# Attention scores of two heads at once, in the two row halves of the array, and block loops written out

## The chip, the core and the metric

The kernel runs on one core of a Trainium2 chip. The metric is the device time of one launch in microseconds (us); the kernel before takes 2647.19 us, the median of three runs (2647.19 to 2650.35). A core has TensorE (PE in the profile; its weight loads are shown apart as PEld), VectorE (DVE), ScalarE (ACT), GpSimd (POOL) and SyncE (SP, which issues the DMAs here). Each runs its own instructions in its own order, and they wait for each other by semaphores. TensorE reads SBUF and writes PSUM, which has 8 banks of 512 float32 values per partition.

## The reference

Two layers, 1024 tokens, model width 1024, heads of 64 channels. Each layer:

```
h = rms_norm(x);  q, k, v = h @ w_in               (three groups of heads)
A: 4 heads, neighbourhood of 8 x 16 on a 16 x 64 grid, learned relative bias
B: 6 query heads on 2 key/value heads, +-128 tokens, ALiBi, a sink per head
C: 6 heads, windows 128, 512, 2048 with dilation 1, 4, 16, ALiBi, mixed by softmax denominators
x = x + concat(rms_norm(A), rms_norm(B), rms_norm(C)) @ w_out
x = x + (silu(h @ w_gate) * (h @ w_up)) @ w_down     (h = rms_norm(x), hidden width 2816)
```

q and k are RMS-normalised per head. For a head, scores = q k^T / 8 + bias, masked; p = softmax(scores); output = p v. All is float32.

## The kernel before

A layer has three parts: the projections, the attention, and output projection with feed-forward part. The change is in the attention, which runs through bodies of tiles. A tile is one head with 128 queries. Four bodies of 24 tiles do the dilated branches 16 and 4 of C (kinds c3 and c2). Then come eight blocks of 128 tokens of 16 tiles each: tiles 0 to 5 are the heads of B, 6 to 11 those of C (dilation 1), 12 to 15 those of A. The first block (b0) and the last (b7) have narrower key windows: 256 keys for B and A and 192 for C, where the six inner blocks have 384 and 256. `plan` lists the bodies; `run` emits them, and the inner blocks 2 to 5 come from a hardware loop (Fori), with their addresses worked out in registers.

A tile goes through these steps:
- `score` (TensorE, L1984): one float32 matmul, queries stationary, keys moving, into a PSUM slot. The trace shows each float32 matmul as two (load, matmul) pairs. QK holds the transposed q and k, two heads of 64 channels in the 128 partitions. The full 128 rows are contracted, so the other head's half of the queries has to be zero: QS holds copies of the queries with zeros in it. For the blocks GpSimd makes these copies (`stage`, L1815); they count up the semaphore `staged`. There are two score slots of two banks (`score2`).
- `tmin` (VectorE, L1381): table minus score, with the row's minimum, into T.
- `exponential` (ScalarE, L1007): in T.
- `unit` (TensorE, L2000): two or three 128 x 128 transposes of T, into bank 4 or 5 by turns. It waits until the unit two before it has been copied out of that bank. For each block but the first, four more units transpose the normalised output Y of the block before: at tiles 8, 9, 11 and 15.
- `copy_unit`: copies bank 4 to PT (VectorE, L1517) or bank 5 (ScalarE, L1019); for Y to QK (L1521, L1023).
- `weigh` (TensorE, L2022): two matmuls of 65 columns per 128 keys, into bank 6 or 7.

The order is written out by hand. TensorE's `pe_body` does for tile s: the score of tile s + 2, the units of tile s, the weighted sum of tile s - 2. VectorE's does for tile s: the copy, the minimum of tile s + 2, then a piece of side work for the block before (`late_finish`, `own_finish`: merging the branches of C, denominators, squares for the norm). ScalarE's does the exponential of tile s + 1, then the copy of tile s. GpSimd raises the mean squares to the power -1/2 (`mean_powers`, L1822), between its copies.

Of the kernel before, what the change touches and what calls it, by code (L numbers as in the profile page):

```python
# [19 lines left out]
P = 128  # L20


def build_program(nc, x, gains, w_in, rpb, w_out, w_gu, w_down, out):
    depth, D = w_in.shape[0:2]
    S = x.shape[1]
    MT = S // P
# [38 lines left out]
    with ctx:  # L65
# [90 lines left out]
        QS = sb("QS", [P, 16, P], F32, "Q")  # L156
# [46 lines left out]
        score2 = [psum[:, 1024 * i:1024 * i + 1024] for i in range(2)]  # L203
# [104 lines left out]
        with nc.Fori(0, depth) as l, ExitStack() as layer:  # L308
# [170 lines left out]
            for kind, rounds, b0 in (("c3", 2, 0), ("c2", 2, 0), ("b0", 1, 0), ("mid", 5, 1), ("b6", 1, 6),  # L479
                                     ("b7", 1, 7)):  # L480
                bd = body(kind, b0, t0, u0, g0, q0)
                nt, nu = n_tiles(bd), len(events(bd))
                ng, nq = (4, 8) if kind in ("c3", "c2") else (3, 6)
                plan.append((bd, rounds, (nt, nu, ng, nq)))
                t0, u0, g0, q0 = t0 + rounds * nt, u0 + rounds * nu, g0 + rounds * ng, q0 + rounds * nq
# [11 lines left out]
            def run(eng, program):  # L497


                for n, entry in enumerate(plan):  # L500
# [5 lines left out]
                    elif dilated(entry[0]):  # L506
                        program(entry[0], shifted(entry, 1), before)
                        program(shifted(entry, 1), after, entry[0])
                    else:
                        program(entry[0], shifted(entry, 1), before)  # L510
                        with loop(eng, 1, rounds) as r:
                            program(shifted(entry, r), shifted(entry, r + 1), shifted(entry, r - 1))
# [13 lines left out]

            def keys(bd, s):

                k, b, (w, _) = bd["kind"], bd["i"], width(bd, s)
                if k == "c3":  # L530
                    return [KS[:, s // 6 % 2, s % 6 // 2, 0:128]]
                if k == "c2":
                    return [KS[:, s // 6 % 2, s % 6 // 2, 0:192]]
                if s < 6:
                    return [QK[:, T_BK, bass.ds(0 if k == "b0" else b * P - P, w)]]
                if s < 12:
                    return [QK[:, T_CK + (s - 6) // 2, bass.ds(0 if k == "b0" else b * P - 64, w)]]
                return [QK[:, T_AK + (s - 12) // 2, bass.ds(0 if k == "b0" else b * P - P, w)]]
# [707 lines left out]
            def _(dve):  # L1246
# [111 lines left out]
                def tmin(bd, s, gate):  # L1358
# [21 lines left out]
                    tt, sc = T[:, s % 4, off:off + w], score2[s % 2][:, 0:w]  # L1380
# [387 lines left out]
            def _(pool):  # L1768
# [15 lines left out]
                def stage(bd, before, q, after_powers):  # L1784

                    k, i = bd["kind"], bd["i"]
                    nh = 4 if q == 2 and not dilated(bd) else 6
                    q2 = q % 2 if dilated(bd) else q

                    if dilated(bd) and q >= 2:  # L1790
                        pool.wait_ge(scored, bd["T"] + 6 * (q - 1))
                    elif before is not None:
                        last = 6 * q + 18 if dilated(before) else 6 * q + nh
                        pool.wait_ge(scored, before["T"] + min(last, n_tiles(before)))
# [4 lines left out]
                    after_powers()  # L1799
                    carrier()  # L1800
                    if dilated(bd):
                        dst = QS[64:128, 6 * q2 + 1:6 * q2 + 7:2, :]
                        kd = KS[:, q2, :, :]
                        if k == "c3":
                            dst = dst.rearrange("p t (r j) -> p t r j", r=2)
                            kd = KS[:, q2, :, 0:128].rearrange("p t (r j) -> p t r j", r=2)
                        g.tensor_copy(dst, dilated_rows(bd, T_CQ, q, P)[64:128]).then_inc(staged, 1)
                        pool.wait_ge(staged, done + 1)
                        carrier()
                        g.tensor_copy(kd, dilated_rows(bd, T_CK, q, 192)).then_inc(staged, 1)  # L1810
                    else:
# [6 lines left out]
                def mean_powers(fam, b, copies):  # L1818
                    pool.wait_ge(gvar_s[fam], b + 1)
                    pool.wait_ge(staged, copies)  # L1820
# [4 lines left out]
                def pool_body(bd, nxt, before):  # L1825

                    b = bd["i"]
                    if dilated(bd):
                        first = bd["kind"] == "c3" and before is None
                        for q in range(4):  # L1830
                            stage(bd, before, q, (lambda: pool.wait_ge(v_ones, 3 if bd["kind"] == "c2" else 2))
                                  if q == 0 else (lambda: None))
                            if first and q == 1:
                                pool.wait_ge(stat, 2 * QT)
                                pool.wait_ge(staged, 4)
                                g.memset(VC[0:64, 0, :, :], 0.0).then_inc(v_ones, 1)
                        return
                    if bd["kind"] == "b0":
                        pool.wait_ge(qk_s, 2 * QT)

# [360 lines left out]
```

## Time and profile before

| | |
|---|---|
| median of 3 runs | 2647.19 us |
| the profiled execution | 2648.14 us, span 2646.4 us |
| granted TensorE clock, mean | 0.981 of full speed |
| busy: PE, DVE, ACT, POOL | 95%, 65%, 41%, 21% of the span |
| attention blocks, layer 1 | about 370 to 555 us |
| one inner block | about 24 us |

The profile page gives each engine's busy time over the whole span, which mixes stages with different limits. Timelines give the start and duration of instructions, those of one line in a row taken together; the durations of matmuls overlap, so that the distance between starts, not the duration, is what a step costs. In brackets stands the idle time ahead of an instruction, and what ended it.

### The profile page before, as it was taken

The numbers are of one execution on the slowest core, as the hardware profiler recorded it, in microseconds if no ns is written. First come the engines' busy times: TensorE is split into PE (matmuls) and PEld (weight loads), VectorE is DVE, ScalarE is ACT, GpSimd is POOL, SyncE is SP. The second block draws the span as 40 slices with busy tenths as digits, with TensorE's granted clock in tenths as the row PEclk, the third lists the DMA queues.
The fourth block names the chain that finished last, engine by engine and source line by source line (L and its number), as shares of the span: only waits on it lengthen the run. The fifth ranks groups of instructions, "written<-read, shape, count | busy, mean of one in ns | idle before, by whom it ended". The sixth has DMA issues, their size and how long they took to land.

```text
span 2646.4 us, 37474 instructions
## 1 busy us (share of the span) xinstructions
PE 2514.2 (95%) x12576; PEld 2109.7 (80%) x12576; DVE 1732.3 (65%) x3358; ACT 1074.3 (41%) x2138; POOL 563.7 (21%) x510
## 2 busy tenths in 40 slices
PE   6999899989899999999989999999898999999997
PEld 5987788878688888878778878888687888888786
DVE  4388667763855555689844986677547555556896
ACT  3333655553522232334343336555444222223342
POOL 1000222100444444200000003221004545441000
PEclk9999999989999999999989999999899999999999
DMA  4311520022222221612232115100331222227023
GB/s 179 94 46 40 120 66 19 13 104 84 80 72 92 76 80 48 224 71 92 68 127 84 44 39 130 51 17 19 107 107 58 86 82 86 61 59 278 13 92 120
DMA packets 229528, 220.19 MB, mean 83 GB/s; under 512 B 48880, under 2 KB 190576, under 8 KB 229360
## 3 DMA queue, kind: packets, MB, share of 16 engines
q1 hardware_dynamic: 229360, 218.07, 26.1%
q8 instruction: 90, 1.47, 0.2%
q14 instruction: 78, 0.64, 0.1%
HBM read 169.96 MB, written 48.06 MB: 82 GB/s over the span
## 4 chain that ended last, share of the span: by engine, by line
PE 45%; DVE 3%; ACT 1%; issue 1%; POOL 0%; DVEq 0%; ACTq 0%; POOLq 0%
PE psum L2121 15%; PE psum L1900 6%; PE psum L1902 6%; PE psum L1901 6%; PE psum L1984 4%; PE psum L2022 3%; PE psum L2000 2%; DVE X L1703 0%; DVE OPL_t L1632 0%; DVE XN L1267 0%; DVE WL L1626 0%; PE psum L2078 0%; PE psum L1948 0%; PE psum L1949 0%; PE psum L1913 0%
## 5 line engine op out<-in xcount | busy, mean ns | idle before, releaser
L2121 PE MATMUL psum<-OPH_t,WH 128*128 128x512 f32 x704 | 276.7, 393 | 17.0 <-DVE WL L1626 7.5
L2121 PE MATMUL psum<-OPH_t,WL 128*128 128x512 f32 x704 | 275.7, 392 | 0.0
L2121 PE MATMUL psum<-OPL_t,WH 128*128 128x512 f32 x704 | 275.6, 392 | 0.0
L1626 DVE TENSOR_TENSOR WL<-RAW,WH 128x512 fp32r<-128x512 f32 x132 | 162.4, 1230 | 160.3 <-ACT WH L1140 160.3
L1900 PE MATMUL psum<-BH,AH 128*128 128x512 f32 x616 | 242.1, 393 | 11.3 <-DVE BL L1695 10.8
L1901 PE MATMUL psum<-BL,AH 128*128 128x512 f32 x616 | 240.9, 391 | 0.0
L1902 PE MATMUL psum<-BH,AL 128*128 128x512 f32 x616 | 240.9, 391 | 0.0
L1007 ACT ACTIVATE T<-T,G 128x192 f32<-128x192 f32 (+3 forms) x352 | 166.3, 473 | 170.4 <-DVE G L1381 167.1
L1870 POOL TENSOR_TENSOR WS<-RAW 128x512 f32<-128x512 f32 x88 | 157.5, 1790 | 238.5 <-PE psum L1902 195.6
L2121 PE MATMUL psum<-OPH_b,WH 128*128 128x512 f32 x528 | 205.8, 390 | 0.0
L2121 PE MATMUL psum<-OPH_b,WL 128*128 128x512 f32 x528 | 205.7, 389 | 0.0
L2121 PE MATMUL psum<-OPL_b,WH 128*128 128x512 f32 x528 | 205.6, 389 | 0.0
L1626 DVE TENSOR_TENSOR WL<-WS,WH 128x512 fp32r<-128x512 f32 x176 | 144.6, 822 | 83.0 <-ACT WH L1140 82.8
L1900 PE MATMUL psum<-PH,HH 128*128 128x384 f32 (+1 forms) x512 | 190.0, 371 | 3.7 <-DVE HL L1594 3.5
L1984 PE MATMUL psum<-QK,QS 128*128 (+3 forms) x512 | 190.3, 453 | 0.9 <-DVE G L1381 0.9
L1901 PE MATMUL psum<-PL,HH 128*128 128x384 f32 (+1 forms) x512 | 187.5, 366 | 0.0
L1902 PE MATMUL psum<-PH,HL 128*128 128x384 f32 (+1 forms) x512 | 187.3, 366 | 0.0
L1900 PE MATMUL psum<-HH,UH 128*128 128x512 f32 x448 | 176.3, 393 | 5.9 <-DVE QK L1311 4.6
L2000 PE MATMUL psum<-ident,T 128*128 128x128 f32 x920 | 178.9, 278 | 2.8 <-ACT T L1007 2.6
L1517 DVE COPY PT<-psum 128x256 f32<-128x256 f32 (+2 forms) x238 | 101.7, 427 | 119.6 <-PE psum L2000 118.6
L1901 PE MATMUL psum<-HL,UH 128*128 128x512 f32 x448 | 175.7, 392 | 0.0
L1902 PE MATMUL psum<-HH,UL 128*128 128x512 f32 x448 | 175.7, 392 | 0.0
(214 smaller groups left out, 5569.8 us busy)
## 6 DMA issues: line engine op xcount, KB each, us to landing
RAW<-in_w_gu SPq DMA_DIRECT2D x176, 256.0 KB, 3.8
WDS<-in_w_down SPq DMA_DIRECT2D x88, 256.0 KB, 2.6
UR<-in_w_in SPq DMA_DIRECT2D x56, 256.0 KB, 3.2
g_mid<-GRES SPq DMA_DIRECT2D x28, 512.0 KB, 2.6
WDK<-in_w_down SPq DMA_DIRECT2D x44, 256.0 KB, 6.6
x_res<-X SPq DMA_DIRECT2D x2, 4096.0 KB, 13.7
PR<-in_w_out SPq DMA_DIRECT2D x32, 256.0 KB, 4.1
X<-x_res SPq DMA_DIRECT2D x2, 4096.0 KB, 13.2
```

What stands on the lines that cost most here:

```text
L1007: a.activation(T[:, s % 4, off:off + w], T[:, s % 4, off:off + w], ACT.Exp, scale=-1.0, bias=G[:, 6 * V1 + place_:6 * V1 + place_ + 1]).th ...
L1517: v.tensor_copy(PT[:, ev[0] % 4, c0:c0 + w], bank[4][:, 0:w]).then_inc(pt_copied[0], 1)
L1626: v.tensor_tensor(WL[SLOT[i, j]][:, :, :], w_source(i, j), WH[SLOT[i, j]][:, :, :].bitcast(F32), ALU.subtract).then_inc(w_lo, 1)
L1870: g.tensor_tensor(WS[i][:, :, :], first, second, op).then_inc(w_sum, 1)
L1900: t.matmul(dst, sh, mh, start=start, stop=False)
L1901: t.matmul(dst, sh, ml, start=False, stop=False)
L1902: return t.matmul(dst, sl, mh, start=False, stop=stop)
L1984: last = t.matmul(score2[slot][:, 512 * j:512 * j + w], QS[:, s % 12 if dilated(bd) else s, :], kk, start=True, stop=True)
L2000: last = t.transpose(dst[0:src.shape[-1], P * i:P * i + P], src, ident[:, :])
L2022: last = t.matmul(group_bank(bd, s)[:, place_ * V1:place_ * V1 + V1], PT[0:n, s % 4, P * c:P * c + P], values(bd, s, c, n), start=(c == 0) ...
L2121: last = t.matmul(dst[:, :], w[SLOT[i, j]][:, k, :], h[o][:, k, :], start=(i in (1, 5, 6) and k == 0 and part == 0), stop=(i in (2, 3, 4) ...
```

## The change

Three things. The scores in the eight blocks no longer contract 128 rows against zero-padded queries: `score_pair` issues the matmuls of heads s and s + 1 behind each other, one in rows 0 to 63 and the other in rows 64 to 127, with queries and keys both read from QK; each has a PSUM bank of its own (`scores`, four banks). Each still counts `scored` up. TensorE's `pe_body` now steps through the blocks two tiles at a time: pair s + 2 and s + 3, the units of s and s + 1, the weighted sums of s - 2 and s - 1. GpSimd's copies for the blocks go, QS shrinks to 12 tiles, and the inverse roots of all blocks form one plain sequence on GpSimd. The inner blocks 1 to 6 are written out one by one on every engine. The dilated bodies keep their way of scoring. VectorE's and ScalarE's order is the same.

```diff
-            for kind, rounds, b0 in (("c3", 2, 0), ("c2", 2, 0), ("b0", 1, 0), ("mid", 5, 1), ("b6", 1, 6),
+            for kind, rounds, b0 in (("c3", 2, 0), ("c2", 2, 0), ("b0", 1, 0), *(("mid", 1, b) for b in range(1, 7)),
                                      ("b7", 1, 7)):
...
+            def heads_rows(bd, s):
+
+                return slice(0, P) if dilated(bd) else slice(64 * (s % 2), 64 * (s % 2) + 64)
+
+            def queries(bd, s):
+
+                if dilated(bd):
+                    return QS[:, s % 12, :]
+                t = T_BQ + s // 2 if s < 6 else T_CQ + (s - 6) // 2 if s < 12 else T_AQ + (s - 12) // 2
+                return QK[heads_rows(bd, s), t, bd["i"] * P:bd["i"] * P + P]
...
+            def scores(bd, s):
+
+                return bank[2 * (s % 2) if dilated(bd) else s % 4][:, 0:width(bd, s)[0]]
...
-                    else:
-                        t0_ = (T_BQ, T_CQ, T_AQ)[q]
-                        qt = QK[:, t0_:t0_ + nh // 2, bass.ds(i * P, P)]
-                        for par in (1, 0):
-                            g.tensor_copy(QS[64 * par:64 * par + 64, 6 * q + par:6 * q + nh:2, :],
-                                          qt[64 * par:64 * par + 64]).then_inc(staged, 1)
...
+                def score_pair(bd, s):
+
+                    if bd["kind"] == "b0" and s == 0:
+                        pe.wait_ge(qk_s, 2 * QT)
+                        pe.wait_ge(tmin_s, bd["T"] - 1)
+                    else:
+                        pe.wait_ge(tmin_s, bd["T"] + s - 2)
+                    for h in range(2):
+                        t.matmul(scores(bd, s + h), queries(bd, s + h), keys(bd, s + h), start=True,
+                                 stop=True).then_inc(scored, 1)
...
-                    for s in range(nt):
-                        if s + 2 < nt:
-                            score(bd, s + 2)
-                        elif nxt is not None:
-                            score(nxt, s + 2 - nt)
+                    step = 1 if dilated(bd) else 2
+                    for s in range(0, nt, step):
+                        to, at_ = (bd, s + 2) if s + 2 < nt else (nxt, s + 2 - nt)
+                        if to is not None and dilated(to):
+                            score(to, at_)
+                        elif to is not None and at_ % 2 == 0:
+                            score_pair(to, at_)
                         for idx, ev in enumerate(evs):
-                            if ev[0] == s:
+                            if s <= ev[0] < s + step:
                                 unit(bd, idx, ev, bd["i"] - 1)
-                        if s >= 2:
-                            weigh(bd, s - 2)
-                        elif prev is not None:
-                            weigh(prev, n_tiles(prev) + s - 2)
+                        for done in range(s - 2, s - 2 + step):
+                            if done >= 0:
+                                weigh(bd, done)
+                            elif prev is not None:
+                                weigh(prev, n_tiles(prev) + done)
```

TensorE around tiles 8 and 9 of an inner block. T is the tile, Y the normalised output, PT the transposed exponentials. Before:

```order
L1984 MATMUL psum<-QK,QS 128x256 [waits tmin_s]
L2000 MATMUL psum<-ident,T 128x128 [waits pt_copied_dve,exp_s]
L2000 MATMUL psum<-ident,T 128x128
L2000 MATMUL psum<-ident,Y 128x128 [waits pt_copied_act,y_s_b]
L2000 MATMUL psum<-ident,Y 128x128
L2022 MATMUL psum<-VC,PT 128x65 [waits grp_s,pt_copied_dve]
L2022 MATMUL psum<-VC,PT 128x65
L1984 MATMUL psum<-QK,QS 128x256 [waits tmin_s]
L2000 MATMUL psum<-ident,T 128x128 [waits pt_copied_dve,exp_s]
L2000 MATMUL psum<-ident,T 128x128
L2000 MATMUL psum<-ident,Y 128x128 [waits pt_copied_act,y_s_b]
```

The same place now, ahead of it the pair of tiles 10 and 11:

```order
L1971 MATMUL psum<-QK 128x256 [waits tmin_s]
L1971 MATMUL psum<-QK 128x256
L1987 MATMUL psum<-ident,T 128x128 [waits pt_copied_dve,exp_s]
L1987 MATMUL psum<-ident,T 128x128
L1987 MATMUL psum<-ident,Y 128x128 [waits pt_copied_act,y_s_b]
L1987 MATMUL psum<-ident,Y 128x128
L1987 MATMUL psum<-ident,T 128x128 [waits pt_copied_dve,exp_s]
L1987 MATMUL psum<-ident,T 128x128
L1987 MATMUL psum<-ident,Y 128x128 [waits pt_copied_act,y_s_b]
L2009 MATMUL psum<-VC,PT 128x65 [waits grp_s,pt_copied_dve]
L2009 MATMUL psum<-VC,PT 128x65
```

The second tile's score has moved up to the first's, and the transposes of tile 9 and their wait for VectorE's copies now follow those of tile 8 and Y, with no weighted sum and no score in between.

GpSimd in the looped inner block, before (grstd is the inverse root; the rows named ISA and REGISTER_ALU work out addresses):

```order
L1822 TENSOR_TENSOR grstd<-gvare,neghalf 128x1 [waits staged]
L1794 ISA
L1815 ISA [waits grstd_s_b,scored,staged]
L1815 COPY QS<-QK 64x3x128
L1815 ISA
L1815 COPY QS<-QK 64x3x128
L1820 REGISTER_ALU [waits gvar_s_a]
L1822 TENSOR_TENSOR grstd<-gvare,neghalf 128x1 [waits staged]
L1822 TENSOR_TENSOR grstd<-gvare,neghalf 128x1 [waits gvar_s_c,staged]
```

Now, for one block:

```order
L1817 TENSOR_TENSOR grstd<-gvare,neghalf 128x1 [waits gvar_s_b]
L1817 TENSOR_TENSOR grstd<-gvare,neghalf 128x1 [waits gvar_s_a]
L1817 TENSOR_TENSOR grstd<-gvare,neghalf 128x1 [waits gvar_s_c]
L1817 TENSOR_TENSOR grstd<-gvare,neghalf 128x1 [waits gvar_s_b]
L1817 TENSOR_TENSOR grstd<-gvare,neghalf 128x1 [waits gvar_s_a]
```

Only the inverse roots are left in the blocks; the copies and their waits for scores are gone.

## Rows read from the trace of the kernel before

**Rows 1.** Busy time of the engines over five inner blocks, clock, DMA

```profile
core 0: us, PE busy (x) PEld busy (x) DVE busy (x) ACT busy (x) POOL busy (x), PEclk, DMA share, GB/s
412.48:533.65 121.17, 121.17 (x832) 101.12 (x832) 95.44 (x371) 68.90 (x156) 23.24 (x45) 1.00 0.06 17
```

**Rows 2.** Waits, 412 to 534 us: total us, times, longest

```profile
ACT T L1007 <- DVE G L1381: 35.5, 37, 1.8
DVE PT L1517 <- PE psum L2000: 20.4, 30, 1.2
...
```

**Rows 3.** Page, costliest groups: busy us, mean ns, idle before, releaser

```profile
L1984 PE MATMUL psum<-QK,QS 128*128 (+3 forms) x512 | 190.3, 453 | 0.9 <-DVE G L1381 0.9
```

**Rows 4.** Timeline of TensorE in an inner block: start, us, instruction

```profile
466.93 0.49 PE L2000 MATMUL psum<-ident,T 128*128 128x128 f32 x3
...
474.52 0.78 PE L2022 MATMUL psum<-VB,PT 128*128 x6
475.13 0.65 PE L1984 MATMUL psum<-QK,QS 128*128 x2
475.62 0.38 PE L2000 MATMUL psum<-ident,T 128*128 128x128 f32 x2
...
476.06 0.56 PE L2022 MATMUL psum<-VC,PT 128*128 x4
...
476.94 0.38 PE L2000 MATMUL psum<-ident,T 128*128 128x128 f32 x2
...
477.82 0.86 PE L1984 MATMUL psum<-QK,QS 128*128 x2
478.52 0.38 PE L2000 MATMUL psum<-ident,T 128*128 128x128 f32 x2
```

**Rows 5.** Timeline of TensorE in the dilated stage, 192 keys

```profile
347.06 0.55 PE L1984 MATMUL psum<-KS,QS 128*128 128x192 f32 x2
347.44 0.38 PE L2000 MATMUL psum<-ident,T 128*128 128x128 f32 x2
```

**Rows 6.** Timeline of TensorE's weight loads in the dilated stage

```profile
346.01 0.30 PEld L1984 LDWEIGHTS psum<-KS,QS 128*128 128x128 f32 x2
...
346.56 0.53 PEld L2022 LDWEIGHTS psum<-VR,PT 128*128 128x128 f32 x4
347.00 0.30 PEld L1984 LDWEIGHTS psum<-KS,QS 128*128 128x128 f32 x2
...
347.55 0.67 PEld L2022 LDWEIGHTS psum<-VR,PT 128*128 128x128 f32 x4
348.29 0.30 PEld L1984 LDWEIGHTS psum<-KS,QS 128*128 128x128 f32 x2
```

**Rows 7.** TensorE's matmuls on 64 rows, whole span: count, busy us, mean ns

```profile
L2022 PE MATMUL psum<-VR,PT 64*128 64x65 f32 x96 | 20.8, 297 | 0.0
```

**Rows 8.** Timeline of VectorE in the same block

```profile
467.46 0.56 DVE L1517 COPY PT<-psum 128x384 f32<-128x384 f32 x1 [0.69 <-PE psum L2000]
467.93 0.54 DVE L1381 CUSTOM_DVE_ANT_0 T<-TB,psum 128x384 f32<-128x384 f32 x1
...
476.32 0.42 DVE L1517 COPY PT<-psum 128x256 f32<-128x256 f32 x1
...
478.94 0.42 DVE L1517 COPY PT<-psum 128x256 f32<-128x256 f32 x1
```

**Rows 9.** Timeline of ScalarE in the same block

```profile
468.52 0.62 ACT L1007 ACTIVATE T<-T,GB 128x384 f32<-128x384 f32 x1 [1.40 <-DVE GB L1381]
...
482.16 0.47 ACT L1019 ACTIVATE PT<-psum 128x384 f32<-128x384 f32 x1
```

**Rows 10.** TensorE's first score behind each inner block

```profile
460.97 0.86 PE L1984 MATMUL psum<-QK,QS 128*128 x2
...
509.63 0.86 PE L1984 MATMUL psum<-QK,QS 128*128 x2
533.65 0.65 PE L1984 MATMUL psum<-QK,QS 128*128 128x256 f32 x2
```

More of the change, by code:

```diff
@@ L202, in build_program @@
         bank = [psum[:, 512 * i:512 * i + 512] for i in range(8)]
-        score2 = [psum[:, 1024 * i:1024 * i + 1024] for i in range(2)]
         with ExitStack() as setup:
@@ L482, in build_program @@
                 nt, nu = n_tiles(bd), len(events(bd))
-                ng, nq = (4, 8) if kind in ("c3", "c2") else (3, 6)
+                ng, nq = (4, 8) if kind in ("c3", "c2") else (3, 0)
                 plan.append((bd, rounds, (nt, nu, ng, nq)))
@@ L525, in width @@
                 return (256 if k in ("b0", "b7") else 384), 0
-            def keys(bd, s):
[L529 to L538, printed above, removed]
+            def heads_rows(bd, s):
[5 more added lines that the diff above has]
+                return QK[heads_rows(bd, s), t, bd["i"] * P:bd["i"] * P + P]
+            def keys(bd, s):
+                k, b, (w, _), rows = bd["kind"], bd["i"], width(bd, s), heads_rows(bd, s)
+                if dilated(bd):
+                    return KS[rows, s // 6 % 2, s % 6 // 2, 0:w]
+                t = T_BK if s < 6 else T_CK + (s - 6) // 2 if s < 12 else T_AK + (s - 12) // 2
+                first = 0 if k == "b0" else b * P - (64 if 6 <= s < 12 else P)
+                return QK[rows, t, first:first + w]
+            def scores(bd, s):
+                return bank[2 * (s % 2) if dilated(bd) else s % 4][:, 0:width(bd, s)[0]]
             def table(bd, s):
@@ L1379, in tmin @@
                     acc = G[:, 6 * V1 + place_:6 * V1 + place_ + 1]
-                    tt, sc = T[:, s % 4, off:off + w], score2[s % 2][:, 0:w]
+                    tt, sc = T[:, s % 4, off:off + w], scores(bd, s)
                     v.tensor_tensor_reduce(out=tt, in0=table(bd, s), in1=sc,
@@ L1782, in carrier, with stage @@
                     pool.sem_inc(pool_gate, 1)
[L1784 to L1790, printed above, removed]
+                def stage(bd, before, q):
+                    i, q2 = bd["i"], q % 2
+                    if q >= 2:
                         pool.wait_ge(scored, bd["T"] + 6 * (q - 1))
                     elif before is not None:
-                        last = 6 * q + 18 if dilated(before) else 6 * q + nh
-                        pool.wait_ge(scored, before["T"] + min(last, n_tiles(before)))
+                        pool.wait_ge(scored, before["T"] + 6 * q + 18)
                     done = bd["Q"] + 2 * q
@@ L1825, in pool_body @@
                 def pool_body(bd, nxt, before):
[L1827 to L1836, printed above, removed]
-                        return
-                    if bd["kind"] == "b0":
-                        pool.wait_ge(qk_s, 2 * QT)
-                    powers = bd["kind"] != "b0" and not (isinstance(b, int) and b == 1)
-                    if powers:
-                        mean_powers(1, b - 2, bd["Q"])
-                    stage(bd, before, 0, (lambda: pool.wait_ge(grstd_s[1], b - 1)) if powers else (lambda: None))
-                    if powers:
-                        mean_powers(0, b - 2, bd["Q"] + 2)
-                        mean_powers(2, b - 2, bd["Q"] + 2)
-                    stage(bd, before, 1, (lambda: pool.wait_ge(grstd_s[2], b - 1)) if powers else (lambda: None))
-                    stage(bd, before, 2, lambda: None)
+                    if not dilated(bd):
+                        return
+                    for q in range(4):
+                        stage(bd, before, q)
+                        if before is None and q == 1:
+                            pool.wait_ge(stat, 2 * QT)
+                            pool.wait_ge(staged, 4)
+                            g.memset(VC[0:64, 0, :, :], 0.0).then_inc(v_ones, 1)
                 pool.wait_ge(qk_s, 2 * T_BQ)
+                pool.wait_ge(v_ones, 2)
                 run(pool, pool_body)
-                for b in (MT - 2, MT - 1):
+                for b in range(MT):
                     for fam in (1, 0, 2):
-                        mean_powers(fam, b, plan[-1][0]["Q"] + 6)
+                        mean_powers(fam, b)
                 def weight_sums(j):
```

40 lines of the change are left out of this document (14 added, 26 removed).

## The prediction

> **What bounds the kernel now.** I read the busy time of each engine by stretches first, then the waits, then single steps of the block stage. In the block stage (some 370 to 555 us of the first layer, and again in the second) TensorE has no idle time at all, at the full clock: 121.17 of 121.17 us over five inner blocks, with VectorE busy for 95.44, ScalarE for 68.90 and GpSimd for 23.24 [rows 1]. The list of waits for the same blocks is headed by those of VectorE and ScalarE for TensorE and for each other [rows 2]; no matmul of TensorE stands in it. So a microsecond taken from or added to TensorE in a block moves the end, as long as VectorE (79% busy) can keep up. The score matmuls are 190.3 us of busy time in 512 records, two for each of the 256 float32 products of the blocks in two layers [rows 3].
>
> **What one score costs.** From the start of a score to the start of the transposes behind it: 477.82 to 478.52, 0.70 us, for 384 keys; 475.13 to 475.62, 0.49 us, for 256 [rows 4]; 347.06 to 347.44, 0.38 us, for 192 [rows 5]. These are two passes of width-proportional time and a constant: 0.70 = 2 x 0.32 + 0.06, 0.49 = 2 x 0.216 + 0.06, 0.38 = 2 x 0.16 + 0.06. An inner block has ten scores of 384 and six of 256, an edge block (first and last) ten of 256 and six of 192.
>
> **Splitting the array has a price, and the trace shows it.** In the dilated stage some weighted sums use 64 rows of the array instead of 128 [rows 7]. The weight loads of a step with 128 rows throughout start at 346.56 and the next score's load at 347.00, 0.44 us for four loads; in the step where two of the four use 64 rows it is 347.55 to 348.29, 0.74 us [rows 6]. Whole steps take 0.99 us (346.01 to 347.00) and 1.29 us (347.00 to 348.29) [rows 6]. Going to 64 rows and back thus costs 0.28 to 0.30 us: a load for another row split starts only when the matmul before it has drained, 0.15 us later each way. Nowhere else in the blocks does TensorE change its split today. After the change it does so sixteen times a block: into the half rows ahead of each of eight pairs, and out again ahead of the transposes. On the way out one thing more is uncovered: today the identity's load starts with the second score pass and lies under it; behind a split it starts after the drain and takes about 0.11 us (the spacing of such loads, 0.44 for four). I take 0.15 + 0.15 + 0.11 = 0.41 us a pair; the lower bound is the measured round trip, 0.28, and zero if the change of split to two halves behaves unlike the one in the trace; the upper, with the boundary between the two heads draining as well, is 0.41 + 0.15 + 0.11 = 0.67.
>
> **What a pair costs after it.** The instructions come as head 0 pass 1, pass 2, head 1 pass 1, pass 2. Two matmuls of one half must follow each other. If matmuls begin in program order, as all rows here do, and the halves work at once, only head 0's second pass and head 1's first can overlap: three passes, not two. With W for a pass (0.32, 0.216, 0.16), a pair costs 0.06 + nW + 0.41 against 4W + 0.12 now:
> n = 3: 384 keys 1.43 for 1.40 (+0.03), 256 keys 1.12 for 0.98 (+0.14), 192 keys 0.95 for 0.76 (+0.19).
> n = 2: 1.11 (-0.29), 0.90 (-0.08), 0.79 (+0.03).
> n = 4 (no overlap): 1.75 (+0.35), 1.33 (+0.35), 1.11 (+0.35).
> No row of this trace has two halves at work together, so n is the unknown; I take 3.
> For n = 3 an inner block (five pairs of 384, three of 256) costs 5 x 0.03 + 3 x 0.14 = +0.57, an edge block (five of 256, three of 192) 5 x 0.14 + 3 x 0.19 = +1.27. Twelve inner and four edge blocks in two layers: +6.8 and +5.1 us.
>
> The Trainium skill, TensorE: Matmul & The Clock Gate, section Part 3: Packing small matmuls, says that matmuls of different row groups run at once, about 4 ns apart, and also that matmuls start and end strictly in program order. By its span rule alone a pair would be n = 2, a result near no change; with its order rule and the two passes that this trace shows it is n = 3. No row here can decide.
>
> **The transposes of two tiles in one step.** The second price is in the order. A transposition waits until the copy two units before it has emptied its PSUM bank. Today a weighted sum and a score stand between the transposes of tile 8 (with Y's) and of tile 9, 476.06 to 476.94 [rows 4]. Now the transposes of both, and those of the normalised output Y, follow each other directly. At four places in a block with Y work three units or more share one step:
> - Tile 9 needs VectorE's copy of tile 8. Tile 8's transposes start at 475.62, the copy starts at 476.32 and takes 0.42 [rows 4, 8], so it ends 1.12 us later; at the least 0.42 + 0.42 = 0.84 (478.52, copy 478.94) [rows 4, 8]. TensorE arrives after two units of 0.22, at 0.44. It stalls 0.46 to 0.74 with 0.06 for the semaphore; I take 0.6.
> - Y's second unit needs ScalarE's copy of the first: 0.1.
> - Y's unit in the step of tiles 10 and 11 needs VectorE's copy of tile 10: 0.84 + 0.06 - 0.44 = 0.46.
> - Y's last unit, behind tiles 14 and 15 (three chunks, 0.33 each, so TensorE arrives at 0.66), needs ScalarE's copy of tile 14: 0.53 until a copy can start (466.93 to 467.46) and 0.47 for it, + 0.06: 0.4 [rows 4, 8, 9].
> Together 1.6 us, and I take 1.5, since the drains ahead give the copies a little time, in each of the seven blocks with Y work, fourteen in all, +21 us. The bounds are 0.5 (if the drains give the copies time and only the longest stall is left) and 2.2 (each of the four 0.15 longer).
>
> **VectorE.** Its work is not changed. 95.44 us in five blocks is 19.1 a block against a block of some 26, so it doesn't become the bound; but around tiles 4 to 8 it runs without a gap, and the second tile of a pair wants its exponential earlier than before. From the first transpose of a 384 step (466.93): VectorE's copy begins at 0.53, its first minimum at 1.0, side work at 1.5, the second minimum would begin at 2.0, and the exponential (0.62) behind it end at 3.2 [rows 4, 8, 9]. TensorE comes for it one step and one tile's transposes later: a tile takes 0.70 + 0.33 + 0.61 now, so a step 3.3 and the sum 3.65 with n = 3, 3.35 with n = 2. That leaves 0.45 or 0.15, and only tile 5 has side work that exceeds it. I count 0.1 us a block, 1.4 us; 0.4 with n = 2.
>
> **What goes.** GpSimd's copies of the queries go. They are hidden under TensorE's work: the list of waits [rows 2] has no engine waiting for them, so the gain is nothing. With them goes the wait for the staging semaphore. The four score banks take away waits for the minimum, which held the score matmuls up for 0.9 us in all [rows 3]. Of the loop, two looped blocks take 460.97 to 509.63 = 24.33 each, and the same work outside the loop 509.63 to 533.65 = 24.02 [rows 10]: 0.3 a round, eight looped rounds in two layers, -2.4 us. Whether the longer program has to wait for its instructions no row tells; I take nothing, and the loop's 2.4 us given back as the other end. GpSimd's inverse roots (L1822) stay as they are.
>
> **The sum** for n = 3: 6.8 + 5.1 + 21 + 1.4 - 2.4 = +32 us. The profiled execution took 2648.1 us (a span of 2646.4 and 1.7 around it), so its like would take 2680; the median of the runs is 0.9 below it, which makes 2679 us.
>
> **Rivals.**
> - No overlap of the halves (n = 4), so that the change doesn't do what it says. Inner 8 x 0.35 = 2.8, edge 2.8: 16 x 2.8 = 45, with 21 - 2.4 it is +64: 2711 us. For it: no row shows an overlap of anything but loads with matmuls. Against: the halves share no rows.
> - Full overlap (n = 2): inner 5 x -0.29 + 3 x -0.08 = -1.7, edge 5 x -0.08 + 3 x 0.03 = -0.3; 12 x -1.7 + 4 x -0.3 = -21.6; + 21 + 14 x 0.4 - 2.4 = +3: 2650 us. For it: the halves share neither rows nor banks. Against it: the order of the passes, since head 1's first stands behind head 0's second.
> - Faster: the halves cost no drain. Then with n = 3 a pair is 0.06 + 3W: 1.02 (-0.38), 0.71 (-0.27), 0.54 (-0.22); inner -2.7, edge -2.0, in all -40; + 21 for the copies, + 5.6 for VectorE, which is then nearly level with TensorE, - 2.4: 2631 us. It wins from the point where a change of split costs less than some 0.16 us a pair (32 us over the 128 pairs of two layers is 0.25, and 0.41 - 0.25 = 0.16). For it: only one kind of split change, at 65 columns, is in the trace. Against it: the step that rows 6 show pays in full.
> The chances: 0.50, 0.27, 0.11 and 0.12. What a measurement of this kernel can tell from no change is about 0.2%, 5 us. The third case falls mostly within it; the first leaves a little for faster and same if the copies cost half. Faster 0.15, within 0.2% 0.10, slower 0.75. The range reaches from the middle of the third and fourth case to just beyond the second: 2640 to 2718; the likeliest case's own range is 2662 to 2689: stalls of 0.5 or 2.2 a block are 14 x -1.0 = -14 or 14 x 0.7 = +10 us, and 0.28 for the change of split is 128 x -0.13 = -17.
>
> **What would show it.** Start to start from a pair's first pass to the transposes: 1.4 us for 384 keys says n = 3, 1.1 says 2, 1.75 says 4. The pair's loads starting 0.2 us or more behind the last weighted sum's matmul say that the drain is paid. TensorE with idle time in the blocks, ended by VectorE's and ScalarE's copies at tiles 9, 11 and 15, says that the order costs what I put down; a block of some 26.4 us instead of 24.3 confirms the sum. The prediction is wrong if blocks are shorter than now, or if TensorE waits mostly for exponentials (then VectorE sets the pace), or if the granted clock falls below 1.00 in the blocks, which I have not counted.

## The result, and the profile after

The changed kernel takes 2657.01 us (median of 5 runs, 2653.48 to 2662.77), the kernel before 2647.19 beside it (2646.44 to 2650.35): a ratio of 1.0037 with a 95% interval of 1.0024 to 1.0050. It is slower, by 10 us, where 32 us more were forecast (2679). The profiled execution took 2653.48 us with a span of 2651.7. Below, the first line of the page, its row of granted clock (40 slices of 66 us) and the two lines of costly groups that answer to [rows 3].

```profile
span 2651.7 us, 36100 instructions
PEclk9999999989999999999999999999799999999999
L1987 PE MATMUL psum<-ident,T 128*128 128x128 f32 x920 | 177.0, 291 | 15.6 <-DVE PT L1525 10.1
L1971 PE MATMUL psum<-QK 64*128 64x384 f32 (+2 forms) x512 | 103.7, 477 | 0.0
```

The score matmuls are as many as before, 512, but TensorE is busy with them for 103.7 us where it was 190.3 [rows 3]. The transposes of T wait 15.6 us, where they waited 2.8. Those two numbers don't make the result: busy time counts a matmul's tail that lies under the next instruction, and leaves out the gaps at a change of split. What a block costs is read from the start of one block to that of the next. TensorE's first pair of four blocks, start and duration:

```profile
458.27 0.92 PE L1971 MATMUL psum<-QK 64*128 64x384 f32 x4
...
482.75 0.92 PE L1971 MATMUL psum<-QK 64*128 64x384 f32 x4
...
507.23 0.92 PE L1971 MATMUL psum<-QK 64*128 64x384 f32 x4
...
531.71 0.70 PE L1971 MATMUL psum<-QK 64*128 64x256 f32 x4
```

An inner block takes 24.48 us, where [rows 10] had 24.33 and 24.02 and the forecast 26.4. With scores in half the time, a block is 0.2 us longer. The busy time of the engines, in the columns of [rows 1]: a stretch of nearly four inner blocks, then the first 16.1 us of the last block in layer 1 and layer 2, then what follows in layer 2.

```profile
413.00:509.00 96.00, 90.08 (x651) 68.09 (x650) 73.50 (x292) 52.02 (x121) 6.57 (x12) 1.00 0.06 18
531.70:547.80 16.10, 14.44 (x109) 11.31 (x108) 12.10 (x57) 9.19 (x24) 1.10 (x2) 1.00 0.00 1
1844.30:1860.40 16.10, 14.44 (x109) 11.31 (x108) 12.10 (x57) 9.19 (x24) 1.09 (x2) 1.00 0.00 1
1860.00:1890.00 30.00, 21.14 (x80) 16.13 (x80) 15.62 (x51) 15.48 (x33) 2.34 (x4) 0.51 0.13 41
```

TensorE had no idle time in the blocks [rows 1]; now it is idle for 5.92 of 96 us. And in layer 2 the granted clock falls to its lower level (0.50 of full speed) at 1860.4, inside the last block, for 30.7 us. In layer 1 it falls only at 559.9, 28 us after the last block's first score and behind its last tile, for 13.7 us, much as in both layers of the kernel before (561.4 and 1872.1, 13.7 us). The same instructions in the two layers' last blocks:

```profile
548.20 0.48 PE L1971 MATMUL psum<-QK 64*128 64x256 f32 x1
...
549.04 0.66 PE L1987 MATMUL psum<-ident,T 128*128 128x128 f32 x4
```

```profile
1861.07 0.79 PE L1971 MATMUL psum<-QK 64*128 64x256 f32 x1
...
1862.63 1.11 PE L1987 MATMUL psum<-ident,T 128*128 128x128 f32 x4
```

The four transposes take 1.11 us for 0.66. From the first block to the output projection (its first matmul) it is 199.20 us in layer 1 and 205.48 in layer 2; before it was 198.42 in both. That is 7.8 us more, while the two profiles' spans differ by 5.3: the stretches that the change doesn't touch went 2.5 us the other way, so a few us between two single profiles can't be read.

What TensorE waits for, over the same 96 us (waiting instruction, what ended the wait, total us, times, longest):

```profile
DVE PT L1525 <- PE psum L1987: 18.8, 20, 2.3
PEld psum L1987 <- issue: 14.1, 27, 0.6
PEld psum L1987 <- ACT T L1015: 10.8, 24, 0.9
PE psum L1987 <- DVE PT L1525: 4.3, 8, 0.7
```

("issue" is time in which the load waited for nothing that the profile shows; the weight loads have gaps that cost nothing.) Two kinds stand here that [rows 2] had not: the transposes wait for VectorE's copies, 8 times, that is twice a block, as forecast for tiles 9 and 11; and the loads of the identity wait for ScalarE's exponentials (T), which was forecast at next to nothing. Of the 5.92 us in which no matmul runs, 5.3 end with a copy (4.3 VectorE's, 1.0 ScalarE's). TensorE from tile 8 on:

```profile
473.44 0.70 PE L1971 MATMUL psum<-QK 64*128 64x256 f32 x4
474.07 0.44 PE L1987 MATMUL psum<-ident,T 128*128 128x128 f32 x2
474.34 0.38 PE L1987 MATMUL psum<-ident,Y 128*128 128x128 f32 x2
475.41 0.41 PE L1987 MATMUL psum<-ident,T 128*128 128x128 f32 x2 [0.69 <-DVE PT L1525]
475.74 0.30 PE L1987 MATMUL psum<-ident,Y 128*128 128x128 f32 x1
475.88 1.06 PE L2009 MATMUL psum<-VC,PT 128*128 128x65 f32 x8
476.87 0.92 PE L1971 MATMUL psum<-QK 64*128 64x384 f32 x4
477.71 0.66 PE L1987 MATMUL psum<-ident,T 128*128 128x128 f32 x4
478.76 0.41 PE L1987 MATMUL psum<-ident,Y 128*128 128x128 f32 x2 [0.39 <-DVE PT L1525]
...
484.82 0.52 PE L1987 MATMUL psum<-ident,Y 128*128 128x128 f32 x3 [0.34 <-ACT PT L1027]
```

The stalls of 0.69 at tile 9, 0.39 at tile 11 and 0.34 at tile 15 are those of the forecast (0.6, 0.46, 0.4). But a pair of 384 keys takes 476.87 to 477.71, 0.84 us to its transposes, where n = 3 said 1.4, and one of 256 takes 473.44 to 474.07, 0.63.

### The profile page after: what moved, and what is told of

The parts are those of the page before. It is cut to its first block and busy times, and to the rows that moved or that the text cites. A ratio compares the mean times of both kernels' runs of the same rounds, so it can differ in the third digit from the quotient of the medians.

```text
span 2651.7 us, 36100 instructions
## 1 busy us (share of the span) xinstructions
PE 2500.8 (94%) x12576; PEld 2069.7 (78%) x12576; DVE 1723.5 (65%) x3358; ACT 1068.0 (40%) x2138; POOL 515.1 (19%) x414
## 5 line engine op out<-in xcount | busy, mean ns | idle before, releaser
L1881 PE MATMUL psum<-BH,AH 128*128 128x512 f32 x616 | 242.4, 394 | 11.2 <-DVE BL L1703 10.8
L1987 PE MATMUL psum<-ident,T 128*128 128x128 f32 x920 | 177.0, 291 | 15.6 <-DVE PT L1525 10.1
L1987 PEld LDWEIGHTS psum<-ident,T 128*128 128x128 f32 x920 | 108.2, 143 | 90.2 <-ACT T L1015 50.9
```

Of the source, the lines that this page charges most:

```text
L1881: t.matmul(dst, sh, mh, start=start, stop=False)
L1987: last = t.transpose(dst[0:src.shape[-1], P * i:P * i + P], src, ident[:, :])
```

## The experiments

Every kernel is compared with the kernel before on the same chip; ratios are to it, with 95% intervals. "Block" is the time from an inner block's first score to that of the next.

**1. The written-out blocks alone.** In the kernel before:

```diff
-... ("mid", 5, 1), ("b6", 1, 6),
+... *(("mid", 1, k) for k in range(1, 7)),
```

> The kernel before with the inner blocks written out and nothing else. Theory A (the clock fell in the last block of layer 2 because TensorE had become less busy; writing out is harmless): blocks of about 24.0 us as the sixth block has now, no low clock inside the blocks, about 2645 us. Theory B (the longer program is what costs the 10 us, by late instructions): about 2657 us and blocks longer than 24.2.

Measured: 2645.29 us (2641.34 to 2647.80, 11 runs) beside 2645.89 (27 runs of the kernel before), ratio 0.9997 [0.9988, 1.0006]. A step of it, and the same place one block later:

```profile
481.75 0.49 PE L2000 MATMUL psum<-ident,T 128*128 128x128 f32 x3
482.07 0.56 PE L2022 MATMUL psum<-VC,PT 128*128 128x65 f32 x4
482.47 0.86 PE L1984 MATMUL psum<-QK,QS 128*128 128x384 f32 x2
...
506.71 0.86 PE L1984 MATMUL psum<-QK,QS 128*128 128x384 f32 x2
```

24.24 us (482.47 to 506.71) against 24.29 on average in the loop. The written-out blocks are worth 0.6 us in the medians, which can't be told from nothing (the interval reaches from 3.2 us less to 1.6 more), and the slower time lies in the rest. Later comparisons of blocks are with this kernel: 24.24 us, and 198.0 from the first block to the output projection.

**2. Pairs, but transposes and weighted sums by turns.** In the changed kernel, for each pair:

```diff
-for idx, ev in enumerate(evs):
-    if s <= ev[0] < s + step:
-        unit(...)
-for done in range(s - 2, s - 2 + step):
-    weigh(done)
+for own in range(s, s + step):
+    for idx, ev in enumerate(evs):
+        if ev[0] == own:
+            unit(...)
+    weigh(own - 2)
```

> The changed kernel, but behind each pair of scores tile s has its transposes and its weighted sum of s-2 before tile s+1 has its own. Theory A (the pair itself gains 2.6 us a block and the transposes of two tiles behind each other lose 3): an inner block of 21.5 to 22.5 us instead of 24.5, waits for the copies almost gone, 14 blocks x 2.5 us less: about 2615 us. Theory B (VectorE's chain of minimum and exponential sets the pace whatever the order): blocks stay at about 24 us and the total at 2645 to 2655.

Measured: 2639.5 us (2634.76 to 2644.1), ratio 0.9973 [0.9964, 0.9982]: faster than before. The block takes 23.37 us, between the two theories:

```profile
484.72 0.92 PE L1971 MATMUL psum<-QK 64*128 64x384 f32 x4
...
508.08 0.92 PE L1971 MATMUL psum<-QK 64*128 64x384 f32 x4
```

TensorE's waits for copies fall from 4.3 + 1.0 us in 96 to 1.6, but those of its loads for exponentials don't (10.8 and 12.1). The order of the changed kernel costs 24.48 - 23.37 = 1.11 us a block, and it alone turned a gain into a loss.

**3 and 4. The same two orders with 128 rows.** Both heads' rows are contracted in every score, so that the result is a sum over two heads; orders and banks stay as in the changed kernel and in experiment 2.

```diff
-return slice(0, P) if dilated(bd) else slice(64 * (s % 2), 64 * (s % 2) + 64)
+return slice(0, P)
```

> The changed kernel's order with all 128 rows in each score (queries of both heads of a tile pair and keys of both, so that the scores are the sum of two heads: the zeroing is left out). No split of the array, no overlap, same stalls. A score pair takes 1.40 us for 384 keys instead of 1.00, so a block is 24.0 + 1.5 to 2.5 = 25.5 to 26.5 us and the total about 2665 to 2680 us. If the clock fell through the half-used array, it stays up in the blocks here; if through TensorE's idle time, it falls in some block here too.

> All 128 rows in each score (sum of two heads as scores, the zeroing left out), pairs of scores, but the transposes and weighted sums of the two tiles by turns as in the run e2. No split, no stalls: a block of about 24.0 us, total about 2645 us, like e1. If it is well above, the pairing of the scores costs something by itself.

Measured: 2669.14 us, ratio 1.0090 [1.0075, 1.0106], in the changed order; 2646.55 us, 1.0002 [0.9993, 1.0011], by turns. Two block starts of the first of them (438.67 and 464.71), between them the start of its last step, and its 96 us:

```profile
438.67 1.51 PE L1971 MATMUL psum<-QK 128*128 128x384 f32 x4
...
461.87 1.51 PE L1971 MATMUL psum<-QK 128*128 128x384 f32 x4
...
464.71 1.51 PE L1971 MATMUL psum<-QK 128*128 128x384 f32 x4
```

```profile
413.00:509.00 96.00, 91.41 (x617) 76.05 (x615) 68.13 (x273) 49.91 (x115) 5.62 (x11) 1.00 0.05 14
```

26.04 us a block, and 24.39 by turns (461.44 to 485.83 in its timeline). So the half rows gain 1.56 us a block in the changed order and 1.02 by turns. They do what the change says. Experiment 4 has everything else that the change brings (pairs, four score banks, written-out blocks, no copies by GpSimd), and its time is that of the kernel before: these parts are worth nothing that shows.

**5. Both heads in the same half.** Every score reads rows 0 to 63, so that half the heads are computed from another head's rows.

```diff
-... slice(64 * (s % 2), 64 * (s % 2) + 64)
+... slice(0, 64)
```

> The changed kernel with both heads of a pair scored from rows 0 to 63 (the odd heads' scores are those of the even ones: their own q and k are left out). If the overlap seen in the changed kernel comes from the two row halves, the four passes now follow each other: start to transposes 4 x 0.32 + 0.2 = 1.5 us for 384 keys instead of 0.84, and a block of 24.5 + 5 x 0.64 + 3 x 0.43, less up to 2 us of waits that it hides, = 27 to 29 us. If the hardware interleaved them for another reason, 24.5 stays.

Measured, one run: 2709.4 us beside 2647.88; the block takes 27.93 us. A whole step of TensorE with no wait in it, and the start of the next:

```profile
468.42 1.55 PE L1971 MATMUL psum<-QK 64*128 64x384 f32 x4
469.91 0.87 PE L1987 MATMUL psum<-ident,T 128*128 128x128 f32 x6
470.62 1.00 PE L2009 MATMUL psum<-VC,PT 128*128 128x65 f32 x8
471.55 1.55 PE L1971 MATMUL psum<-QK 64*128 64x384 f32 x4
473.04 0.87 PE L1987 MATMUL psum<-ident,T 128*128 128x128 f32 x6
```

From the pair to its transposes 1.49 us, against 0.84 in different halves: 0.65 less, two passes of 0.32. So this stretch is 0.20 + nW, with n = 4 in one half and n = 2 in two. The whole step takes 3.13 us (468.42 to 471.55), the same step on 128 rows 2.84 (461.87 to 464.71 in experiment 3): 0.29 for changing the split. The start times of the records, read one by one in the changed kernel, show how: the two heads' first passes start at 462.072 and 462.079 us, their second ones at 462.499 and 462.506. The Trainium skill, TensorE: Matmul & The Clock Gate, Part 3: Packing small matmuls, gives starts about 4 ns apart in different row groups; these are 7 ns apart, and the second passes also go side by side. Only the later two of the four count `scored` up, so they are the second passes of the two heads, and both first passes start ahead of both.

**6. The last block alone on 128 rows, from experiment 2.** GpSimd copies the last block's queries into the zero-padded tiles during the first block, as it did for all blocks before; the last block's scores use them.

```diff
-return slice(0, P) if dilated(bd) else ...
+return slice(0, P) if dilated(bd) or bd["kind"] == "b7" else ...
+if bd["kind"] == "b7":
+    return QS[:, s, :]
```

> The run e2 with the last block alone scored on all 128 rows against zero-padded queries that GpSimd copies during the first block. By the block times of e4 and e2 that costs 1.0 us a layer. Theory A (half-used rows in the last block let the clock fall there): the mean granted clock goes from 0.977 back to about 0.981, no low clock before the end of the last block, and the total to 2639.5 + 2 - 8 = about 2633 us. Theory B (the clock falls through the half rows of all blocks, and would fall elsewhere): clock stays at 0.977 and the total goes to 2641.

Measured: 2632.82 us (2627.87 to 2633.78), ratio 0.9934 [0.9920, 0.9947]. From the first block to the output projection it takes 191.07 and 191.02 us in the two layers; experiment 2 takes 190.17 where the clock stays, and 195.56 where it falls in the last block. The mean clocks of all runs lie apart: 0.975 to 0.979 in the eleven of experiment 2, 0.981 to 0.984 in the five here. That is Theory A.

**7. The minimum first, from experiment 2.** In a block VectorE computes the minimum of tile s + 2 before it copies the transposes of tile s, not behind.

```diff
+if not dilated(bd):
+    tmin(...)   # tile s + 2
 copy_unit(...)
-tmin(...)
```

> The run e2, and in the blocks VectorE takes the minimum of tile s+2 ahead of the copy of tile s instead of behind it (the scores are there a whole tile earlier since the pairs). Theory A (what is left of the gain is lost because the exponentials come late, since VectorE's minimum stands behind a copy that waits for TensorE): TensorE's loads no longer wait for exponentials, an inner block 22.0 us or less instead of 23.37, total about 2620 us. Theory B (VectorE's own work bounds the block): no change, 23.4 us and 2639 us; or longer, since the copies come later.

Measured: 2625.17 us (2616.14 to 2626.59), ratio 0.9898 [0.9881, 0.9915], the block 22.64: it gains, but less than Theory A said, and the loads still wait for exponentials (13.6 us in 96). It beats both kernels. VectorE, ScalarE and the weight loads at one exponential, first in experiment 2 and then here:

```profile
490.86 0.70 PE L1971 MATMUL psum<-QK 64*128 64x256 f32 x4
...
492.08 0.56 DVE L1525 COPY PT<-psum 128x384 f32<-128x384 f32 x1 [0.99 <-PE psum L1987]
...
492.55 0.41 DVE L1389 CUSTOM_DVE_ANT_0 T<-TC,psum 128x256 f32<-128x256 f32 x1
...
493.01 0.51 ACT L1015 ACTIVATE T<-T,G 128x256 f32<-128x256 f32 x1 [1.30 <-DVE G L1389]
```

```profile
483.45 0.70 PE L1978 MATMUL psum<-QK 64*128 64x256 f32 x4
...
484.34 0.42 DVE L1389 CUSTOM_DVE_ANT_0 T<-TC,psum 128x256 f32<-128x256 f32 x1 [0.63 <-PE psum L1978]
...
484.68 0.55 DVE L1525 COPY PT<-psum 128x384 f32<-128x384 f32 x1
484.80 0.51 ACT L1015 ACTIVATE T<-T,G 128x256 f32<-128x256 f32 x1 [0.52 <-DVE G L1389]
```

In the first, VectorE stands idle for 0.99 us until transposes that it is to copy are there, and the minimum behind the copy starts 1.69 us after the pair. In the second the minimum starts 0.89 us after its pair.

**8. Experiments 6 and 7 together.**

> e6 and e7 together. Theory A of both: about 2613 us with the clock at 0.981. If only the order of VectorE counts, as e7; if neither, 2641.

Measured: 2624.2 us (2620.71 to 2626.27), ratio 0.9909 [0.9895, 0.9923]. That is 11 us above the theory, and no difference from experiment 7 can be told, nor in the mean clocks (0.979 to 0.983 in both). The profiled execution, its fastest run, takes 185.63 and 185.66 us in the two layers; experiment 7 takes 184.68 where the clock stays and 191.04 where it falls.

**9 and 10. No transposes of Y in the blocks,** in the changed kernel and in that of experiment 1.

```diff
-if dilated(bd) or bd["kind"] == "b0":
-    continue
+continue   # no unit of Y in any body
```

> The changed kernel without the transposes and copies of Y inside the blocks (the attention output of blocks 0 to 6 is left out; only the last block's goes on). The Y transposes themselves are 8 x 0.11 = 0.9 us a block. Theory A (as I predicted, most of TensorE's new waits come from Y standing between transposes that share a bank): the block falls by 0.9 + about 1.5 us more, from 24.48 to about 22.1. Theory B (most are waits for exponentials): it falls by 0.9 and little else, to about 23.4. To be read against the run e10.

> The same left out of the kernel e1 (one score at a time, written out): it has hardly a wait at those places, so 24.24 - 0.9 = 23.35 us a block under both theories.

Measured, one run each: 2629.28 and 2627.89 us. The blocks of the changed kernel take 22.62 us (459.25 to 481.87 in its timeline), those of the kernel before 23.19 (483.04 to 506.23). Y's units cost 1.86 us a block in the changed order and 1.05 in the old one: 0.81 more, which lies between the 1.5 of Theory A and the nothing of Theory B. What the first of them waits for on TensorE:

```profile
PEld psum L1986 <- ACT T L1014: 16.6, 33, 0.8
...
PE psum L1986 <- ACT T L1014: 4.2, 8, 0.6
```

No wait for a copy is left, and those for exponentials are all there. TensorE is idle for 4.36 of its 96 us (busy for 91.64), and for none in the old order without Y (96.00).

**11. The changed kernel with the last block on 128 rows,** the edit of experiment 6.

> The changed kernel as it is, but the last block scored on all 128 rows against zero-padded queries. Theory A (the granted clock falls in the last block because its scores fill only half of the array, and that is the larger part of the 10 us): clock back to about 0.981 in most runs, and 7 us less than the changed kernel, about 0.1% above the kernel before. Theory B (the clock has another cause, such as TensorE's waits, which stay): clock and time as in the changed kernel, 0.4% above.

Measured: 2652.94 us (2648.41 to 2654.71, 11 runs), ratio 1.0023 [1.0014, 1.0032]. The last block with what follows takes 39.18 us where the changed kernel takes 36.73 undisturbed, so the edit itself costs 2.45 us a layer, 4.9 in all, and yet the kernel isn't slower than the changed one: its mean clocks, 0.980 to 0.983, lie above all of the changed kernel's (0.975 to 0.979). The 7 us that the theory named are 4 in the medians. Not all falls are gone: 17.7 us into the last block the clock is at its lower level for 3.4 us, in both layers, which is in the 2.45, but no fall of the length seen in the changed kernel (30.7) begins before the last tile is done. The first of them:

```profile
551.00:554.40 3.40, 3.22 (x13) 2.36 (x12) 1.51 (x7) 0.78 (x2) 0.00 (x0) 0.50 0.00 0
```

**12. The changed kernel with the minimum first,** the edit of experiment 7.

> The changed kernel (transposes of two tiles behind each other) with VectorE's minimum of tile s+2 ahead of its copy of tile s. Theory A (waits for exponentials are the larger part of the loss): 24.48 falls to about 23 us. Theory B (waits for the copies are the larger part): they get longer by a minimum each, so 24.5 us or more.

Measured: 2658.67 us (2655.04 to 2661.07), ratio 1.0040 [1.0024, 1.0055]. The block takes 24.26 us (459.42 to 483.68), 0.22 less, and the time can't be told from the changed kernel's. The gain of Theory A didn't come. Its waits on TensorE:

```profile
PEld psum L1994 <- ACT T L1015: 12.5, 20, 1.2
PE psum L1994 <- DVE PT L1525: 6.4, 8, 1.0
```

The waits for VectorE's copies grew from 4.3 to 6.4 us, and those for exponentials from 10.8 to 12.5. Minimum first pays 0.73 us a block together with the turns and 0.22 without them.

## Why the prediction was right and wrong

Slower was right, and 2657 lies in its range, but 10 us came where 32 were forecast, the time is outside the likeliest case's own range (2662 to 2689), and what makes it slower is mostly not what I had summed: that the sign is right is in good part luck. Step by step:

**"Only head 0's second pass and head 1's first can overlap" was the step that failed.** It rested on "if matmuls begin in program order". Experiment 5 and the changed kernel give n = 4 and n = 2, never 3; the float32 matmuls go side by side pass by pass, and both first passes start ahead of both second ones (462.072, 462.079; 462.499, 462.506), so that the strict order which the prediction took up doesn't hold between the passes of two matmuls. Two scores of 384 keys cost 1.40 before; a pair was to cost 1.43 and costs 0.35 less than they do, 1.05 with the change of split.

**The price of the split** was 0.41 us a pair and is 0.29. Whole steps of TensorE without a wait and with the same transposes and weighted sums, start to start:

| a pair of tiles | 384 keys | 256 keys |
|---|---|---|
| two tiles of experiment 1 | 3.29 (463.27 to 466.56) | 2.65 (472.80 to 475.45) |
| 128 rows, changed order (3) | 3.29 (494.90 to 498.19) | 2.64 (478.41 to 481.05) |
| one half, changed order (5) | 3.58 (475.99 to 479.57) | 2.93 (486.30 to 489.23) |
| two halves, changed kernel | 2.94 (462.07 to 465.01) | 2.51 (470.93 to 473.44) |
| two halves, by turns (7) | 2.89 (477.67 to 480.56) | 2.46 (486.13 to 488.59) |

One half against 128 rows is 0.29 more at both widths, and the rows of [rows 6] give 0.30: the lower bound. The 0.11 that I had added for an uncovered load isn't there on top. Against two tiles of experiment 1, a pair in the changed kernel takes 0.35 less at 384 keys and 0.14 less at 256, and by turns 0.40 and 0.18. The pairs thus give 5 x 0.35 + 3 x 0.14 = 2.2 us a block (by turns 2.5) where I counted a loss of 0.57. The 0.05 a pair between the two orders, 0.4 a block, is part of the 1.11 of experiment 2 and stands in no wait; with 128 rows it is there too (3.29 and, in experiment 4, 3.24 from 465.01 to 468.25).

**The copies** were 1.5 us a block. The three stalls in the rows above come to 1.42, but a wait for a copy partly takes the place of a wait for an exponential: experiments 9 and 10 make the net price 0.81.

**VectorE and the exponentials** were 0.1 us a block and are 1.6. Without Y the changed order takes 22.62 and the old one 23.19; the pairs give 2.17, so 2.17 - 0.57 = 1.60 is lost to waits that have nothing to do with Y. That they are for exponentials is what the waits of experiment 9 name; 1.03 of it (4.36 us in 96) is time without a matmul, the rest lies under loads that start late, which is argued. In the changed kernel itself the matmuls' own waits are nearly all for copies, so the sign "TensorE waits mostly for exponentials" came true only with the loads. The forecast worked out one tile whose copy was on time and allowed 0.4 a block for n = 2. What it left out is that the copy of tile s itself waits for transposes that now come late, and that the minimum of tile s + 2, whose scores are ready, stands behind it on VectorE. Experiment 7 shows that for the order by turns (0.73 us a block from VectorE's order alone). In the changed order the same edit gives only 0.22; that the late copies take it back is argued from the waits, not shown.

**The loop** was -2.4 us. Measured -0.05 a round, -0.6 in all and not distinguishable from nothing. [rows 10] compared different work: the start at 533.65 stands behind a score of 256 keys, those at 460.97 and 509.63 behind one of 384, and that is 0.21 (0.70 - 0.49) of the 0.31.

A block then is 24.24 - 2.17 + 0.81 + 1.60 = 24.48, the measured time. That is no check: the last two terms are differences of block times and close the sum by construction; only the 2.17 is measured by itself. Side by side: an inner block was to grow by 0.57 + 1.5 + 0.1 = 2.17 us and grows by 0.24. Over a layer, with the first block +0.17, the second -0.2 and five of +0.24, the changed kernel takes 199.20 for 198.0: 2.4 us in two layers.

**The clock** was a term of zero, "not counted", and it is most of the 10 us. In the profiled execution the last block of layer 2 loses 205.48 - 199.20 = 6.3 us to it. Over the runs the time follows it: the mean granted clocks are 0.979, 0.975, 0.979, 0.977 and 0.978 for 2653.48, 2662.77, 2655.07, 2658.91 and 2657.01 us, and 0.981 in the profile of the kernel before. What is left when 2.4 is taken from the measured 9.8 and the 0.6 of the loop added is 8 us, between one such fall and two.

What brings the fall about? Not TensorE's idle time alone. With 128 rows in the same order (experiment 3) TensorE is idle in the blocks too (4.59 of 96 us, against 5.92), and in the same 16.1 us of the last block in layer 2 it is busy for 14.61 us against the changed kernel's 14.44:

```profile
1864.20:1880.30 16.10, 14.61 (x108) 12.96 (x107) 11.66 (x54) 9.02 (x24) 1.10 (x2) 1.00 0.00 1
```

There the clock stays up for another 13 us, and its mean over the runs is 0.981 to 0.983. And in experiment 5, with half rows, few waits and TensorE busy for 18.35 of the 19.50 us ahead of the fall (94%), it falls for 30.7 us in both layers. All profiles sort the same way. With half-row scores in the last block (the changed kernel, 2, 5, 7, 9 and 12) each shows a fall of 27 us or more that begins 14 to 20 us into it, in one layer or both; the mean clocks are 0.973 to 0.979, and 0.979 to 0.983 for experiment 7. Without them (before, 1, 3, 4, 6, 8, 10, 11) none shows more than the 3.4 us of experiment 11 before the last tile is done, and the mean clocks are 0.979 to 0.984. Experiments 6 and 11 changed that block's rows on purpose, and the mean clocks of all their runs lie above those of 2 and of the changed kernel: so the half-row scores there bring the fall about in these two orders. Two things limit it. Wider rows also make the block longer, so no run varied them with everything else exactly equal; and from 7 to 8 the same edit made no difference in time or mean clock that can be told. The trace of the kernel before has half-row matmuls in its last block too, twelve in each layer (L2022, VC, 64x65, 546.65 to 553.93 in layer 1), though the prediction says that TensorE changes its split nowhere in the blocks; with those alone the clock stays. Why it falls in one layer and not in the other, with the same instructions, stays open.

**The rivals.** "Full overlap (n = 2)", at 0.11, was the true mechanism, and its 2650 is 7 us off: it had the gain of the pairs too small (the split at 0.41), the copies too dear, the exponentials too cheap (0.4), and no clock, and these errors cancel; that it comes so near is luck. The rival that the halves don't overlap fell with experiment 5. The one with no drain fell with the measured 0.29 a pair, and its turning point of 0.16 was worked out for n = 3; with n = 2 the split may cost what it does, and the pairs still gain.

## What to carry to other kernels

When one engine's work in a loop gets shorter, recompute each wait behind it at the new pace, and ask of each in-order engine whether an instruction that could run stands behind one that waits: here the paired scores gained 2.2 us a block, and waits that the orders of TensorE and VectorE make took back 2.4. Two tiles' scores may share a step without their transposes doing so; transposes and weighted sums by turns and the minimum before the copy gave 2625 us where the kernel before took 2648 (ratio 0.9898). And matmuls that fill half the rows went with a lower clock here, beside their own time, so after such a change look at the granted clock at the end of each dense stretch, in more than one run.

## What the runs showed of the hardware

- Two float32 matmuls in different row halves, issued behind each other, start 7 ns apart and run both their passes side by side: 0.84 us to the next instructions for two scores of 384 keys, 1.49 when both use one half.
- Going to a half-row split and back costs about 0.3 us of TensorE's time: 0.30 at 65 columns [rows 6], 0.29 at 256 and at 384 (experiment 5 against 3).
- With half-row scores at the end of the blocks the granted clock can fall to its lower level for 27 to 34 us while TensorE is 90% or 94% busy (14.44 of 16.10 us, 18.35 of 19.50), and a fall costs 5.4 to 6.4 us (195.56 - 190.17, 205.48 - 199.20, 191.04 - 184.68). With 128 rows there, at 14.61 of 16.10 us, it fell for 3.4 us in experiment 11 and not at all in 3.
